# Index scores of the prompt taken between the transposes of the row tiles, in PSUM banks of their own

## The reference, cut to what matters

```
dots  = einsum('bqhd,bld->bqhl', qi, kidx) * (D_IDX ** -0.5)     # 16 index heads, D_IDX = 128
score = einsum('bqh,bqhl->bql', wi, relu(dots))                  # summed over the heads
score = where(s <= t, score, NEG);  idx = top_k(score, topk)
```

## Time and profile before

| | |
|---|---|
| time, median of 3 runs | 3191.79 us (3190.94 to 3193.51) |
| profiled execution, its time | 3183.96 us |
| its span, first to last instruction | 3182.3 us |
| granted TensorE clock, mean over the span | 0.949 of 2.4 GHz |
| TensorE busy with matmuls | 2915.3 us, 92% |
| VectorE, ScalarE, GpSimd busy | 1364.8, 716.9, 131.8 us |

### The profile page before, as it was taken

The page is one execution under the profiler, slowest core; times in us unless marked ns, Lnnn a source line. Parts: engine busy times, 40 slices in busy tenths (PEclk is TensorE's granted clock), DMA queues, the critical chain, the costliest instruction groups (busy, mean ns, idle before and its releaser), DMA issues. The chain is left out here.

```text
span 3182.3 us, 56354 instructions
## 1 busy us (share of the span) xinstructions
PE 2915.3 (92%) x22142; PEld 2598.7 (82%) x22142; DVE 1364.8 (43%) x2212; ACT 716.9 (23%) x1082; POOL 131.8 (4%) x150
## 2 busy tenths in 40 slices
PE   7699999999995879998988886996999999999897
PEld 4499999999994459997544565996999999999897
DVE  1422242212242537777661567435433433443434
ACT  2211222111220212221000455223222222221222
POOL 0000031000041000000000000000000000000000
PEclk8799999999997999998996898998999999999898
DMA  9766666776655653333889535431333333333421
GB/s 334 232 189 196 191 212 213 217 221 200 207 173 151 173 163 106 106 108 100 276 260 348 163 120 178 134 90 46 100 104 93 97 95 99 99 92 106 120 81 54
DMA packets 594874, 496.87 MB, mean 156 GB/s; under 512 B 37148, under 2 KB 515885, under 8 KB 593885
## 3 DMA queue, kind: packets, MB, share of 16 engines
q1 hardware_dynamic: 527912, 408.44, 43.6%
q10 hardware_dynamic: 58992, 60.59, 5.8%
q0 software_dynamic: 7840, 26.10, 2.1%
HBM read 460.02 MB, written 48.70 MB: 160 GB/s over the span
## 5 line engine op out<-in xcount | busy, mean ns | idle before, releaser
L146 PE MATMUL psum<-h_high,w_high 128*128 128x260 f32 x4992 | 1009.2, 283 | 21.6 <-DVE w_low L133 21.6
L146 PE MATMUL psum<-h_high,w_low 128*128 128x260 f32 x4992 | 1006.9, 283 | 0.0
L146 PE MATMUL psum<-h_low,w_high 128*128 128x260 f32 x4992 | 1005.2, 283 | 0.0
L146 PEld LDWEIGHTS psum<-h_high,w_high 128*128 128x128 f32 x4992 | 770.4, 189 | 35.9 <-issue 30.1
L146 PEld LDWEIGHTS psum<-h_high,w_low 128*128 128x128 f32 x4992 | 770.7, 189 | 0.0
L146 PEld LDWEIGHTS psum<-h_low,w_high 128*128 128x128 f32 x4992 | 768.9, 189 | 0.0
L133 DVE TENSOR_TENSOR w_low<-w,w_high 128x2048 fp32r<-128x2048 f32 x162 | 371.5, 2294 | 552.3 <-ACT w_high L128 552.3
L128 ACT ACTIVATE w_high<-w 128x2048 fp32r<-128x2048 f32 x162 | 309.1, 1909 | 465.5 <-PE psum L146 361.1
L628 DVE COPY pj_out<-psum 128x260 f32<-128x260 f32 x66 | 28.3, 429 | 382.7 <-PE psum L146 382.7
L576 ACT ACTIVATE pj_out<-psum 128x260 f32<-128x260 f32 x66 | 25.6, 388 | 585.4 <-PE psum L146 585.4
L1047 PE MATMUL psum<-w,cz_xt 128*128 128x256 f32 x512 | 134.5, 404 | 0.0
(11 more groups left out here) (333 smaller groups left out, 2678.2 us busy)
## 6 DMA issues: line engine op xcount, KB each, us to landing
w<-in_w_ada SPq DMA_DIRECT2D x96, 1024.0 KB, 7.8
w<-in_w_in_att SPq DMA_DIRECT2D x65, 1024.0 KB, 11.6
w<-in_w_in_conv SPq DMA_DIRECT2D x64, 1024.0 KB, 6.3
proj<-pj_out POOLq DMA_DIRECT2D x66, 260.0 KB, 4.7
cz_pg<-in_cache_nsa_cmp_k SPq DMA_DIRECT2D x128, 128.0 KB, 2.1
cz_pg<-in_cache_nsa_cmp_v SPq DMA_DIRECT2D x128, 128.0 KB, 2.2
w<-in_w_out_att SPq DMA_DIRECT2D x16, 1024.0 KB, 6.8
w<-in_w_out_conv SPq DMA_DIRECT2D x16, 1024.0 KB, 6.0
```

The lines of the kernel that those rows point to most:

```text
L146: mm = pe.matmul(k.psum[:, banks + hf, 0:HC], w[:, kt, :], x[:, kt, hf * HC:(hf + 1) * HC], start=(kt == 0 and m == 0), stop=(kt == KT - 1 ...
```

## The change

The stage computes the same values from the same inputs. These things differ:

- Entry n is transposed into banks 0 to 2 always. Banks 3 to 7 belong to the scores. A head's matmuls now fill three pieces (128 and 256 columns together, 384, 512), each in the next of these five banks in turn; TensorE waits for the relu of the piece five before.
- ScalarE applies the relu piece by piece, three instructions a head, and raises `relu_done` after each.
- After each entry n = 3 to 9 come two heads on TensorE and, behind the entry's output DMAs, on ScalarE. VectorE adds the two heads of entry n - 1 behind the copies of entry n. Heads 14 and 15 come last. The loops are written out.
- `rw_src` has three buffers, `ip_q` four. SyncE asks for entries 0 to 2, `ip_k`, four query tiles and `sT`, then entries 3 to 9, each behind its waits, with two further query tiles after each from entry 4 on, and then `pages`, `hot` and the weight. Query and key tiles are loaded without the 8 sample columns.
- VectorE's queries come ahead of the adds of heads 12 to 15.

```diff
+    NT, SRC, QR, PIECES, BANKS, FIRST = len(tiles), 3, 4, 3, 5, 3
+    heads_after = {n: [2 * (n - FIRST), 2 * (n - FIRST) + 1] for n in range(FIRST, NT)}
+    last_heads = range(2 * (NT - FIRST), NI)
+    PIECE = [(0, 2), (2, 3), (3, 4)]
...
+        def piece(h, p):
+            i0, i1 = PIECE[p]
+            return ps[:, 3 + (PIECES * h + p) % BANKS, 0:off(i1) - off(i0)]
...
-                for n, (tile, name) in enumerate(tiles):
-                    if n >= 2:
-                        sp.wait_ge(turned, n - 1)
...
+                def load_q(h):
+                    if h >= QR:
+                        sp.wait_ge(mm_done, h - QR + 1)
+                    sp.dma_start(q[:, h % QR, :], k.proj[QI + h, :, 0:T]).then_inc(q_in[h % QR], 16)
+                for n in range(SRC):
+                    load_tile(n)
+                sp.dma_start(ki[:, :], k.proj[KI, :, 0:T]).then_inc(k_in, 16)
+                for h in range(QR):
+                    load_q(h)
+                sp.dma_start(k.sT[:, :, :], k.proj[0:GW, :, T:TC].rearrange("t p s -> p t s")).then_inc(got, 16)
+                for n in range(SRC, NT):
+                    sp.wait_ge(turned, n - SRC + 1)
+                    load_tile(n)
+                    for h in heads_after.get(n - 1, []):
+                        load_q(h + QR)
+                    if n == FIRST + 1:
+                        sp.wait_ge(gated, 2)
+                        sp.dma_start(k.gate_rows, k.gws[:, :]).then_inc(out, 16)
...
+                def scores(h):
+                    pe.wait_ge(q_in[h % QR], 16 * (h // QR + 1))
+                    for p, (i0, i1) in enumerate(PIECE):
+                        n = PIECES * h + p
+                        if n >= BANKS:
+                            pe.wait_ge(relu_done, n - BANKS + 1)
+                        for i in range(i0, i1):
+                            mm = pe.matmul(piece(h, p)[:, off(i) - off(i0):off(i + 1) - off(i0)], q[:, h % QR, i * P:(i + 1) * P], ki[:, 0:P * (i + 1)], start=True, stop=True)
+                    mm.then_inc(mm_done, 1)
...
-                    if n >= 2:
-
-                        pe.wait_ge(kept, 2 * (n - 1))
+                    if n:
+
+                        pe.wait_ge(kept, 2 * n)
...
+                    for h in heads_after.get(n, []):
+                        scores(h)
+                for h in last_heads:
+                    scores(h)
...
+                def relu(h):
+                    act.wait_ge(mm_done, h + 1)
+                    act.wait_ge(added, h + 1)
+                    for p, (i0, i1) in enumerate(PIECE):
+                        nc.scalar.activation(rl[:, h % 2, off(i0):off(i1)], piece(h, p), ACT.Relu, scale=SCALE).then_inc(relu_done, 1)
...
+                for h in last_heads:
+                    relu(h)
...
+                    for h in heads_after.get(n - 1, []):
+                        add(h)
+                queries()
+                for h in heads_after[NT - 1]:
+                    add(h)
+                for h in last_heads:
+                    add(h)
```

More of the change, by code:

```diff
@@ L734, in _ @@
[L734 to L741, removed]
+                        sp.dma_start(src[:, n % SRC, 0, :], k.proj[tile]).then_inc(tile_in[n % SRC], 16)
@@ L756, in _ @@
                             at = i * 256 + g * P
[L757 to L758 removed]
+                            pe.transpose(ps[:, at // 512, at % 512:at % 512 + P], src[:, n % SRC, g, i * P:(i + 1) * P], k.ident)
+                        mm = pe.transpose(ps[0:NS, 2, g * P:(g + 1) * P], src[:, n % SRC, g, T:TC], k.ident)
                     mm.then_inc(turned, 1)
[L760 to L768, removed]
+                    if n == FIRST:
+                        pe.wait_ge(k_in, 16)
+                    for h in heads_after.get(n, []):
+                        scores(h)
+                for h in last_heads:
+                    scores(h)
             @block.scalar
             def _(act):
+                def relu(h):
[3 more added lines that the diff above has]
+                        nc.scalar.activation(rl[:, h % 2, off(i0):off(i1)], piece(h, p), ACT.Relu, scale=SCALE).then_inc(relu_done, 1)
                 act.wait_ge(kept, 2)
@@ L792, in _ @@
                         act.dma_start(k.ga_4[32 * c:32 * c + 32, sh, :], k.gate_rows[4 * sh:4 * sh + 4, 0:NGA].rearrange("s (h b) -> s h b", b=3)).then_inc(back, 16)
-                with act.Fori(0, NI // 2) as j:
-                    for b in range(2):
-                        act.wait_ge(mm_done, j * 2 + (b + 3))
-                        act.wait_ge(added, j * 2 + (b + 1))
-                        for i in range(TT):
-                            ins = nc.scalar.activation(rl[:, b, off(i):off(i + 1)], ps[:, 4 * b + i, 0:P * (i + 1)], ACT.Relu, scale=SCALE)
-                        ins.then_inc(relu_done, 1)
+                for h in last_heads:
+                    relu(h)
@@ L800, in _, with add @@
                 for b in range(2):
-                    act.wait_ge(rows_out[b], 32 * len([n for n in range(1, len(tiles)) if n % 2 == b]))
+                    act.wait_ge(rows_out[b], 32 * len([n for n in range(1, NT) if n % 2 == b]))
             @block.vector
             def _(dve):
+                def add(h):
+                    dve.wait_ge(relu_done, PIECES * (h + 1))
+                    dve.wait_ge(added, h + 2)
+                    for i in range(TT):
+                        ins = dve.scalar_tensor_tensor(out=sc[:, off(i):off(i + 1)], in0=rl[:, h % 2, off(i):off(i + 1)], scalar=k.gw[:, i, NGA + h:NGA + h + 1],
+                                                       in1=sc[:, off(i):off(i + 1)], op0=ALU.mult, op1=ALU.add)
+                    ins.then_inc(added, 1)
@@ new lines, in queries @@
+                def queries():
+                    dve.wait_ge(got, 16)
+                    dve.wait_ge(zero, 2)
+                    for pad, tile in ((k.qpa, QA), (k.qpb, QB)):
+                        for s in range(NS):
+                            at = s * 64 + s % 4 * NH
+                            own = pad[:, at:at + 72].rearrange("p (g h) -> p g h", g=G)[:, :, 0:4]
+                            dve.tensor_scalar(own, k.sT[:, tile:tile + NH, s].rearrange("p (g h) -> p g h", g=G), SCALE, None, ALU.mult).then_inc(step, 1)
+                    for h in range(NI):
+                        dve.tensor_scalar(k.qpi[:, h:h + 144 * 7 + 1:144], k.sT[:, QI + h, :], SCALE, None, ALU.mult).then_inc(step, 1)
```

77 lines of the change are left out of this document (29 added, 48 removed).

## The result

The changed kernel takes 3172.56 us (3168.81 to 3175.93, median of 4 runs) against 3193.51 us (3190.94 to 3196.03, 5 runs) before, measured in turns on one chip: a ratio of 0.9937 [0.9924, 0.9950], 20.9 us or 0.66% faster. The forecast was 3178.9 with a range of 3174 to 3188. One further run of the changed kernel took 4163.49 us at a mean granted clock of 0.643 instead of 0.948 and is left out.

A forecast was written before the change was run, and what follows sets the result against it. First half of the stage bound by DMA, second by TensorE; overlapped, 6.35 us cycles bound by the relu chain. Start, cycles and tail end the stage 12.9 us earlier, later stages 0: 3191.8 - 12.9 = 3178.9 us, range 3174 to 3188.

The forecast's parts named there:

- The cycle: Per entry with two heads: copies, add, relu, last 512-column matmul and next transposes take 6.35 us, relu chain the bound.
- The load cover: In each cycle the next entry's load takes 5.6 us at most and stays hidden by 0.3 to 0.7 us.
- The stall of 2.8 us behind the ten small DMAs: Stage's tail: head 14's relu stands behind ScalarE's ten small DMAs, ending at 1058.7 instead of 1055.5; VectorE idles 2.8 us.
- Loads as the bound: Rival: entries land 7.5 us after issue, the cycle is 8 us, gain 4.7 us, 3187 us; chance 0.13.
- The clock: Rival: TensorE at half clock in the cycles, about 10.9 us each, stage 15 us slower, 3207 us; chance 0.08.
- An overlap that gains nothing: Rival: relu chain so long that cycles and tail equal the two halves, needing 8.9 us a cycle; chance 0.04.
- A next stage with its page loads alone: Case better than the sum: the next stage's page loads run alone, faster; chance 0.03, no size given.
- "12.9 us earlier", for the stage: The changed stage's end, after the barrier: 1065.75 us instead of 1078.62.
- entry 3's landing: Start of stage: entry 3, queued behind `sT`, lands at about 1003.5 us, some 4 us later; bounds 1000 to 1008.
- the likeliest case: Whole kernel: 6.5 to 18 us of gain, 3174 to 3185 us; chance 0.72.
- "The written-out loops cost nothing that a row shows; 0 as well, 1 us either way": Term for writing out the changed stage's loops: counted as 0, 1 us either way.
- "The difference is what I carry over": Profiled execution goes from 3183.96 to 3171.1 us; the 12.9 us difference is taken off the runs' median, 3191.8.

## Why the prediction was too small

**The mechanism was right.** Two halves with opposite limits were laid over each other; with the heads last some 10 to 11 us of the gain are gone. The cycle was forecast at 6.35 us with the relu chain as its bound and came at 6.28, with TensorE's wait where it was said to be, 0.60 instead of 0.7 us. Three relu buffers removed that wait. The load cover, called thin at 0.3 to 0.7 us, was wider: `rw_src` landed a median of 3.7 us after its issue, not 5.6, hence about 2 us of cover for most entries, though only some 0.5 for entry 5 with its 5.1 us. GpSimd was last. The stall of 2.8 us behind the ten small DMAs is there as 2.05 + 0.72.

**The rivals.** Loads as the bound: TensorE's matmuls waited for no `rw_src` after entry 3. The clock: the middle stretch has 1.00, so the prediction's rival did not come. Nor did the rule of the page "TensorE: Matmul & The Clock Gate" of the Trainium skill (A second HAM failure mode: psum-queue depth-cycling), which reports it from another kernel, apply here to five banks in turn with idles of 0.6 us. An overlap that gains nothing is ruled out by the 18 us. A next stage with its page loads alone was not faster: `stage_index_sample` took 67.8 and 71.1 us against 67.4 to 69.6 before.

**"12.9 us earlier", for the stage.** This term was mis-sized: from the profile of before that the forecast read to the profile of after it is 17.0 us (94.1 to 77.1). Counted from the stage's start, in us:

```
                                  forecast   measured
end of the transposes of entry 3      21.4       20.2
of entry 4                            27.8       25.8
of entry 9                            58.9       56.7
end of the last add                   78.6       74.4
next stage's first instruction        81.2       77.1
```

Of the 4.1 us, 1.2 are entry 3's landing, 0.8 the first two heads and the transposes behind them, where TensorE's clock rose sooner than in the earlier trace rows (0.85 of full in the 2 us from 1006 and 1.00 from 1008; 4.74 us for both heads), 0.2 the cycles, and 2.0 the tail, where I had rounded most pieces up: adds of 3.9 to 4.0 us per pair where 4.3 was taken, queries of 2.4 where 3.0 was. All four errors have one sign, so they add up and do not cancel. The prediction's own bounds, 3.5 for the landing, 3 for the cycle and 1 for the relus, make a gain of 20.4 us when they fall together; it let the likeliest case end at 18. On the other side, the stage of before was 93.7 to 95.9 us over its profiles, and the one read was the shortest, another 1 us.

**"The written-out loops cost nothing that a row shows; 0 as well, 1 us either way", for the later stages.** This is the step that failed: a term was put at nothing with no reason beyond the rows that had been looked at. `stage_attend_prompt` gave 3.6 to 5.3 us, about a fifth of the gain. With this term at 4.4 and all else as forecast the sum is 3174.5; with the stage's term at 17.0 and this one at nothing it is 3174.8; with both it is 3170.4. Either correction alone stays inside the range, and both together leave it. The row was there: the waits of before have an idle of 4.6 us on VectorE put down to issue in `stage_attend_prompt`. I did not ask whether a longer stream ahead of it could move it. A bound for it would have been that wait itself, 4.6 us of gain, and the same again as a loss if a stop appears at another loop.

**The sum as measured:** 18.2 for the stage (94.9 to 76.7 as means of the table) and 4.4 for `stage_attend_prompt` is 22.6, less 1 to 4 us by which `stage_index_sample` and `stage_attend_samples` were longer in these profiles, against 18.5 to 20.9 in the two comparisons of medians. Whether those 1 to 4 us are the change's or chance is open; the variants of the changed kernel have 263.3 to 267.4 in `stage_attend_samples`, the profiles of before 263.3 to 266.1, which speaks for chance.

**"The difference is what I carry over", to the median of the runs.** This is sound as a way of carrying a difference over, but the profile read was 8 to 10 us quicker than the median of its kernel, and from one profile I could not say where in the program that was.

## What to carry to other kernels

When two halves of a stage leave free what the other lacks, the gain of interleaving is set by the new chain's turn; work that out hop by hop, and then by the same hops ask what one more buffer would do: here a third relu buffer was worth another 4 us. A load of short rows delays what stands behind it in its queue (here TensorE waited 6.5 and 3.7 us for the next entry at the two places tried), so it belongs behind the last load that someone waits for. And if an edit changes the number of instructions of an engine, look in later stages for idles that no semaphore ends: they can vanish or appear.

## What was not expected of the hardware

- A stop of 3.9 to 4.6 us on VectorE, near the start of a loop's second turn, depends on how many instructions stand ahead of it: gone with 56 more (no such row, the stage 217.8 instead of 221.1 and 221.4 us), back with 256 more (4.5 us, the stage 221.0).
- A bare semaphore increment on VectorE costs about 0.10 us: 200 of them stand in 21.7 us of idle, of which 2.6 are a barrier's; in the kernel before, 56 stand in 6.4 us with 1.4 of barrier, 0.09 us each.
- ScalarE issues DMAs while its own activation runs: the first small DMA stands behind all three relu pieces of head 13 in the program and was issued at 1047.74 us, 0.08 us after the first piece began, and the pieces lasted until 1049.01. With the issues spread, the relus took the same 0.49 us for the first piece and 0.97 us for the other two.
- `sT`, 8320 rows of 32 bytes, landed 7.7 to 11.1 us after its issue, over all twelve profiles and the four places it had in them.
